# Wide unused products in the attention of the second block: with every unit of two query blocks, with none behind them

## The reference

```python
# swa_branch: 128 queries see the keys of their block and of the block before; a sink logit per head
logits = einsum('bnqgrd,bnkgd->bngrqk', qb, kb) * HEAD_DIM ** -0.5
p = softmax(concatenate([where(mask, logits, -inf), sink], -1), -1)[..., :-1]
o_b = einsum('bngrqk,bnkgd->bnqgrd', p, vb)
# dsa_branch: each query attends to its top 128 causal keys, chosen by an index score
logits = where(valid, einsum('bqgrd,bqkgd->bqgrk', qg, ks) * scale, -inf)
o_a = einsum('bqgrk,bqkgd->bqgrd', softmax(logits, -1), vs)
# then
mix = sigmoid(g_a) * (o_a @ w_branch_a) + sigmoid(g_b) * (o_b @ w_branch_b)
x = x + mix @ w_out
```

## Time and profile before

| what | value |
|---|---|
| median of 3 runs | 2536.84 us (2533.47 to 2542.15) |
| the profiled execution, its own time | 2532.14 us |
| its span in the trace | 2530.4 us |
| PE busy | 2410.5 us (95%) |
| PEld busy | 1908.9 us (75%) |
| DVE busy | 1356.2 us (54%) |
| POOL busy | 1116.7 us (44%) |
| ACT busy | 963.0 us (38%) |
| chain that ended last | PE 80%, DVE 10% |

### The profile page before, as it was taken

One profiled execution on the slowest core, in us unless ns is written; L12 is line 12 of the kernel. 1 busy time (PEld: TensorE's weight loads), 2 busy tenths in 40 slices (PEclk: granted clock), 3 DMA queues, 4 the chain that ended last, 5 costly groups with the idle time before them and its releaser, 6 DMA issues.

```text
span 2530.4 us, 29267 instructions
## 1 busy us (share of the span) xinstructions
PE 2410.5 (95%) x10750; PEld 1908.9 (75%) x10750; DVE 1356.2 (54%) x2070; ACT 963.0 (38%) x1526; POOL 1116.7 (44%) x554
## 2 busy tenths in 40 slices
PE   4989799999999999889999999998999999999998
PEld 4866577878888878666777888876775668788887
DVE  6889845873533799974566112265566433412222
ACT  3347443331332335754233223335533432422332
POOL 2578512534434639761263444462431014444443
PEclk7999899989999999999999999999997999999999
DMA  6522102525545423220122323322330003233232
GB/s 236 192 83 69 58 26 82 188 92 183 166 153 171 152 73 101 63 73 26 42 83 80 95 91 100 99 76 72 91 84 26 1 26 100 80 95 99 92 99 75
DMA packets 215222, 239.88 MB, mean 95 GB/s; under 512 B 9738, under 2 KB 188746, under 8 KB 215114
## 3 DMA queue, kind: packets, MB, share of 16 engines
q1 hardware_dynamic: 215114, 238.45, 29.9%
HBM read 236.32 MB, written 2.10 MB: 94 GB/s over the span
## 4 chain that ended last, share of the span: by engine, by line
PE 80%; DVE 10%; issue 2%; ACT 1%; POOL 1%; DMA 0%; DVEq 0%; SPq 0%; ACTq 0%; POOLq 0%
PE product L2245 22%; PE product L2246 21%; PE product L2247 21%; DVE side L1668 5%; PE side L2750 2%; PE product L2321 2%; PE side L2548 1%; PE product L2572 1%; PE product L2772 1%; PE side L2760 1%; PE side L2307 1%; PE side L2314 1%; PE side L2341 1%; PE side L2566 1%; PE product L2341 1%
## 5 line engine op out<-in xcount | busy, mean ns | idle before, releaser
L869 POOL TENSOR_TENSOR ring_low<-ring_f,ring_high 128x1024 fp32r<-128x1024 f32 (+1 forms) x350 | 847.3, 2426 | 1260.0 <-ACT ring_high L978 1259.8
L2245 PE MATMUL product<-slot_r,ring_high 128*128 128x512 f32 x2792 | 1107.5, 397 | 43.5 <-ACT slot_f L1162 9.8
L2246 PE MATMUL product<-slot_r,ring_low 128*128 128x512 f32 x2792 | 1094.2, 392 | 0.0
L2247 PE MATMUL product<-slot_r,ring_high 128*128 128x512 f32 x2792 | 1093.9, 392 | 0.0
L2245 PEld LDWEIGHTS product<-slot_r,ring_high 128*128 128x128 f32 x2792 | 529.0, 189 | 173.5 <-issue 32.7
L978 ACT ACTIVATE ring_high<-ring_f 128x1024 fp32r<-128x1024 f32 (+1 forms) x350 | 367.7, 1054 | 704.2 <-DMA ring_f<-in_w_ff 340.9
L2247 PEld LDWEIGHTS product<-slot_r,ring_high 128*128 128x128 f32 x2792 | 528.5, 189 | 112.6
L2246 PEld LDWEIGHTS product<-slot_r,ring_low 128*128 128x128 f32 x2792 | 529.3, 190 | 110.5 <-issue 1.7
L1634 DVE SCALAR_TENSOR_TENSOR va<-product,sqt 128x512 f32<-128x512 f32 x96 | 66.2, 691 | 354.7 <-ACT sqt L1057 353.1
L1668 DVE SCALAR_TENSOR_TENSOR side<-slot_f,cols,side 128x512 f32<-128x512 f32 x332 | 220.6, 744 | 0.0
L1647 DVE TENSOR_TENSOR slot_f<-product,slot_f 128x512 f32<-128x512 f32 x64 | 44.1, 690 | 184.2 <-PE product L2247 184.2
(11 more groups left out here) (282 smaller groups left out, 2201.4 us busy)
## 6 DMA issues: line engine op xcount, KB each, us to landing
ring_f<-in_w_ff SPq DMA_DIRECT2D x128, 512.0 KB, 3.6
slot_f<-in_w_ada SPq DMA_DIRECT2D x48, 1024.0 KB, 6.1
ring_f<-in_w_in SPq DMA_DIRECT2D x96, 512.0 KB, 3.7
ring_f<-in_w_out SPq DMA_DIRECT2D x40, 512.0 KB, 3.5
ring_f<-in_w_up SPq DMA_DIRECT2D x32, 512.0 KB, 3.7
ring_f<-in_w_down SPq DMA_DIRECT2D x32, 512.0 KB, 3.4
slot_f<-in_x SPq DMA_DIRECT2D x4, 512.0 KB, 9.1
ring_f<-in_w_v SPq DMA_DIRECT2D x4, 512.0 KB, 3.8
```

Of the source, the lines that this page charges most:

```text
L869: pool.tensor_tensor(ring_low[:, s, :, 0:n], ring_f[:, s, :, 0:n], ring_high[:, s, :, 0:n].bitcast(F32), ALU.subtract).then_inc(low_ready. ...
L2245: pe.matmul(out_ap, high, rhs_high, start=start, stop=False)
L2246: pe.matmul(out_ap, low, rhs_high, start=False, stop=False)
L2247: return pe.matmul(out_ap, high, rhs_low, start=False, stop=stop)
```

## The change

`fill(u)` is called for other units. Before, each even unit of all 64 has one (32 calls). After it, each of the units 0 to 15 has one (16 calls), and none of the units 16 to 63. Nothing else differs: no wait, no buffer and no other engine's list.

```diff
@@ TensorE, the loop over the units
                 if u < UNITS:
                     transposes(u)
-                if u < UNITS and u % 2 == 0:
+                if u < UNITS and u < 16:
                     fill(u)
                 if 0 <= u - 1 < UNITS:
                     pv(u - 1)
```

## The result

The changed kernel took 2551.13 us in the median of 15 runs (2543.63 to 2554.87), the kernel before 2542.15 us in the median of 15 (2522.03 to 2551.41). The ratio is 1.0043 with a 95% interval of 1.0023 to 1.0063: slower by some 11 us, where 19.8 us were forecast. The changed kernel's profiled execution took 2550.24 us, with a span of 2548.3 us. An execution more than 1.5% above the fastest of its kernel is left out of the ratios: none here, and in the experiments 2585.68 us of the removed half alone and 2579.36 us of the kernel with fills in the first block and half of the fifth.

A forecast was written before the change was run, and what follows sets the result against it. TensorE's list and its granted clock were taken to set the attention's pace; -5 - 20.6 + 1.3 + 44.1 = +19.8 us gave 2552 us from the profile or 2556.6 us from the median, range 2546 to 2588 us.

The forecast's parts named there:

- The clock falls in the fifth query block: In units 32 to 39, without fills, the clock drops to 0.5 about behind unit 35 and stays down.
- the wait: In the third unit of the fifth query block, TensorE stalls 0.73 us because the work with `block_out` takes too long.
- The rival that it never falls: The attention keeps clock 1.0 without fills: -24 us, 2512.5 us, or 2523 with a late rise; chance 0.15.
- the rule of idle gaps: Skill page's claim that clock drops are avoided by leaving TensorE no idle gaps between matmul bursts; would keep the clock up.
- the thin units: Units 32 to 39: 128, 128 and 64 columns per 0.85 us, the widest contracting over only 64 rows.
- rows 8: Profile rows at 1684.40 to 1687.80: TensorE busy with narrow products for 3.40 us at 1.00, then granted 0.50.
- Which instruction waits: Without fills, transposes wait for ACT's exponential in the third unit of query blocks 2 to 4; +1.3 us in all.
- The price of the low clock: Extra time at clock 0.5 from about unit 35 to the end of the attention: +44.1 us.
- The start: Units 0 to 15 with a fill each: the clock rises about behind unit 3, net -5 us, bounds -7 and +12.
- The fills removed: Units 16 to 62 lose 24 fills at clock 1.0, each 0.86 us and hidden by nothing: -20.6 us.
- Base of the comparison: The +19.8 us was added to the profiled 2532.1 us, giving 2552, or to the median 2536.8, giving 2556.6 us.

The follow-up runs named there:

- the removed half alone: Against the kernel before: fills with the even units 0 to 14 only, none behind; ratio 1.0158 (1.0108 to 1.0208).
- the kernel with unit 34: Against the changed kernel: a single fill more, in unit 34; ratio 0.9889 (0.9854 to 0.9924), attention 118.1 us.

## Why the prediction was right, and where its numbers were off

- **The clock falls in the fifth query block: right.** Forecast behind unit 35, measured in step 37, and in steps 34 and 35 in two other kernels without a fill at the wait. The rival that it never falls was wrong, and with it what the rule of idle gaps gives here (the Trainium skill, page "TensorE: Matmul & The Clock Gate", table "Why this matters for your kernels"): TensorE's longest gap in these units was 0.61 us. The prediction gave two reasons, the thin units and the wait, and the runs do not part them fully. That the clock can fall among the thin units without the wait is seen in one profile, in step 33. That the wait adds to it is argued only, from the fill of unit 34 and from the fall in step 12 of the kernels with fills in the first and fifth block. The support from rows 8 was weaker than the prediction has it: the first 1.3 of the 3.40 us ahead of that fall are still products of 512 columns, and only the rest is narrow.
- **Which instruction waits: wrong in part.** I followed the chain to the exponential and the transposes. The wait comes earlier in the unit, at `qk`, which needs the logits of the unit two before it. The size held: 0.68 us and then 0.20 us more in two steps of the fifth block, 0.24 us in the step ahead of a waiting `qk` in the third (1963.07 - 1961.44 = 1.63 us in place of 1.39), together near the 0.73 and the 0.2 to 0.3 us forecast.
- **The price of the low clock: 44.1 forecast, 40.8 measured** (98.47 us from step 32 on, against 118.12 - 60.46 = 57.66 us in the kernel with unit 34). The sizes of the units at clock 0.5 held (3.57 for 3.60, 4.64 for 4.68 us), which is 0.6 us. A fall up to two units later is at most 1.2 us of the rest; the last 1.5 us stay open.
- **The start: -5 forecast, -7.1 measured**, since the clock rose in step 2 and not behind unit 3.
- **The fills removed: -0.86 us each, as read.** Steps 16 to 31 lost 8 fills (6.9 us), gained some 0.6 us of waits and 0.4 more, -5.9 us in all.
- **Base of the comparison: the step that failed most.** The sum was made against one profile of before. Against that profile the attention grew by 15.9 us and the span by 18.0, for a forecast of +19.8. The kernel before has no single time of the rise: the prediction saw it in unit 12 and took that as given by the order of work, while three profiles have it in steps 8, 13 and 21. In part it is luck that the time itself, 2551.13 us, came so near to the 2552 to 2556.6 us forecast: the median of 2536.8 us that it started from is 5 us below the later one, and the forecast loss is 9 us above the measured one.

## What to carry to other kernels

When products are put in only to hold the clock, put them where the products around are small and another engine makes TensorE wait as well, not evenly: here one at the right place did what eight over the block did, and its absence cost 39 us. One was also close to too few, as the fall in step 33 shows. Read such a stretch by the granted clock, not by the busy share, and take more than one profile of a kernel whose clock rises in the middle of a stage. Before fills are taken out of a stage, look for what else the other engines do there; the selection on DVE made the second block differ from the third.

## What was not expected of the hardware

- Fills that contract over 64 rows and not 128 left the clock at 0.50 for 222 us with TensorE always busy, where whole ones in each unit raised it 5 to 10 us into the attention. At clock 0.5 they took 2.00 us and not 1.71.
- With no gap longer than 0.61 us in the chain of TensorE, the clock fell from 1.00 to 0.50 and stayed there for 92 us. In one kernel it fell with no gap over 0.17 us in the 9 us before.
- The same program met the rise 23, 38 or 65 us into the attention in three executions.
